# Two-block transformer kernel: first weights by k-slices behind the modulation rows, ring loads behind the last row, fourth recurrent gates one unit later

## The reference, cut to what matters

```python
c_act = jax.nn.silu(c)
mod = c_act @ mod_w[l] + mod_b[l]
sh1, sc1, g1, sh2, sc2, g2 = [m[:, None, :] for m in jnp.split(mod, 6, axis=-1)]
h = rms_norm(x, norm1_g[l]) * (1.0 + sc1) + sh1
proj = h @ w_in[l]
```

```python
xr = causal_depthwise_conv(xr, conv_w[l], conv_b[l])
r = jax.nn.sigmoid(block_diag_linear(x, w_a, b_a).astype(jnp.float32))
i = jax.nn.sigmoid(block_diag_linear(x, w_x, b_x).astype(jnp.float32))
log_a = -LRU_C * r * jax.nn.softplus(-lam.astype(jnp.float32))
a = jnp.exp(log_a)
u = jnp.sqrt(-jnp.expm1(2.0 * log_a)) * (i * xf)
```

## Time and profile before

| | |
|---|---|
| median of 3 runs | 3400.48 us (3400.35 to 3402.3) |
| profiled execution | 3401.0 us, of which the span of the profile 3399.3 us |
| TensorE (PE) busy | 3379.3 us, 99% |
| weight loads (PEld) | 2759.7 us, 81% |
| VectorE (DVE) | 1695.2 us, 50% |
| ScalarE (ACT) | 1316.7 us, 39% |
| GpSimd (POOL) | 1806.4 us, 53% |
| mean DMA rate | 100 GB/s; 391 to 426 GB/s from 4.5 to 36 us |

### The profile page before, as it was taken

How to read it: one execution, slowest core, us unless ns; L and a number is a source line. 1 busy time by engine, 2 the same in 40 slices (tenths; PEclk the granted TensorE clock), 3 DMA queues, 4 the chain that set the end, 5 groups by cost and what they waited for, 6 DMA issues and landing times.

```text
span 3399.3 us, 46823 instructions
## 1 busy us (share of the span) xinstructions
PE 3379.3 (99%) x15522; PEld 2759.7 (81%) x15522; DVE 1695.2 (50%) x2556; ACT 1316.7 (39%) x1820; POOL 1806.4 (53%) x2326
## 2 busy tenths in 40 slices
PE   9999999999999999999999999999999999999999
PEld 5888777888888887888888888888887888788887
DVE  8887775544553438614334434544368324243444
ACT  4365664222232226735633222322237545532222
POOL 6444435655555556553355555555556543465554
PEclk9999999999999999999999999999999999999999
DMA  5222552322222233231223223222223222223223
GB/s 218 88 68 69 174 168 99 110 95 99 93 99 94 97 99 106 93 99 63 69 94 106 97 94 99 93 99 96 95 93 118 93 74 69 81 93 99 99 93 111
DMA packets 93563, 339.59 MB, mean 100 GB/s; under 512 B 10497, under 2 KB 10881, under 8 KB 93314
## 3 DMA queue, kind: packets, MB, share of 16 engines
q1 hardware_dynamic: 86690, 313.16, 27.6%
q10 hardware_dynamic: 6752, 24.80, 2.4%
HBM read 331.62 MB, written 2.10 MB: 98 GB/s over the span
## 4 chain that ended last, share of the span: by engine, by line
PE 93%; DVE 3%; DVEq 1%; ACT 1%; DMA 1%; issue 1%; ACTq 0%; SPq 0%
PE ps L491 28%; PE ps L493 27%; PE ps L492 27%; PE ps L657 1%; PE ps L658 1%; PE ps L659 1%; PE ps L970 1%; PE ps L950 1%; PE ps L738 1%; DMA arena<-in_mod_w 1%; DVE arena L2112 1%; PE ps L961 1%; PE ps L598 0%; DVEq L2134 0%; DVE arena L2136 0%
## 5 line engine op out<-in xcount | busy, mean ns | idle before, releaser
L482 POOL TENSOR_TENSOR w_lo<-raw,w_hi 128x256 fp32r<-128x256 f32 x2268 | 1783.9, 818 | 1569.3 <-ACT w_hi L1057 1569.2
L1057 ACT ACTIVATE w_hi<-raw 128x1024 fp32r<-128x1024 f32 x569 | 599.2, 1056 | 1023.0 <-PE ps L493 1006.7
L491 PE MATMUL ps<-a_hi,w_lo 128*128 128x512 f32 x2216 | 875.0, 395 | 0.3 <-DVE a_lo L1773 0.3
L493 PE MATMUL ps<-a_hi,w_hi 128*128 128x512 f32 x2216 | 863.4, 390 | 0.0
L492 PE MATMUL ps<-a_lo,w_hi 128*128 128x512 f32 x2216 | 863.0, 389 | 0.0
L491 PE MATMUL ps<-b_hi,w_lo 128*128 128x512 f32 x2128 | 830.6, 390 | 4.2 <-DVE b_lo L1845 4.0
L492 PE MATMUL ps<-b_lo,w_hi 128*128 128x512 f32 x2128 | 829.1, 390 | 0.0
L493 PE MATMUL ps<-b_hi,w_hi 128*128 128x512 f32 x2128 | 829.0, 390 | 0.0
L491 PEld LDWEIGHTS ps<-a_hi,w_lo 128*128 128x128 f32 x2216 | 416.3, 188 | 98.2 <-issue 13.9
L493 PEld LDWEIGHTS ps<-a_hi,w_hi 128*128 128x128 f32 x2216 | 416.0, 188 | 88.3
L492 PEld LDWEIGHTS ps<-a_lo,w_hi 128*128 128x128 f32 x2216 | 416.5, 188 | 82.6 <-issue 0.5
(11 more groups left out here) (281 smaller groups left out, 2789.0 us busy)
## 6 DMA issues: line engine op xcount, KB each, us to landing
raw<-in_stream SPq DMA_DIRECT2D x570, 512.0 KB, 3.3
arena<-in_mod_w ACTq DMA_DIRECT2D x32, 512.0 KB, 4.0
arena<-in_mod_w SPq DMA_DIRECT2D x16, 512.0 KB, 11.5
arena<-arena ACTq DMA_DIRECT2D x16, 256.0 KB, 3.7
xres<-in_x_t SPq DMA_DIRECT2D x4, 512.0 KB, 5.0
xres<-in_x_t ACTq DMA_DIRECT2D x1, 2048.0 KB, 9.3
out_t<-xres SPq DMA_DIRECT2D x8, 256.0 KB, 2.0
arena<-in_first SPq DMA_DIRECT2D x3, 512.0 KB, 10.7
```

Source lines behind the costliest of these rows:

```text
L482: last = pool.tensor_tensor(w_lo[:, s, part], raw[:, s, part], w_hi[:, s, part].bitcast(F32), ALU.subtract)
L491: pe.matmul(out, lo, x_hi, start=start, stop=False)
L493: return pe.matmul(out, hi, x_hi, start=False, stop=stop)
L1057: act.activation(w_hi[:, slot, :], raw[:, slot, :], ACT.Copy).then_inc(hi_ready, 1)
```

## The change

Three things are changed.

The three first units are stored as eight slices, one for each k, each with the 128 columns of all three units (196,608 bytes). The load of slice k is issued behind the modulation loads 2k and 2k + 1, and TensorE waits for slice k in front of its matmuls for k. The three ring units 0 to 2 are all issued behind the last modulation load and the last slice. ScalarE's code is as it was.

`keep_columns` moves on VectorE from between the fourth and the fifth modulation load to behind the eight subtractions that make `a_lo`.

On TensorE, in each of the two layers, the fourth pair's `lru_gates(3)` moves from in front of the first output-gate tile to between the first and the second. ScalarE and VectorE keep their order.

```diff
-        first_w = area(ARENA - BRANCH, FIRST, D)
+        first_w = area(ARENA - BRANCH, KT, FIRST * P)
...
-        first_loaded, masks_ready, c_spread = sem("first_loaded"), sem("masks_ready"), sem("c_spread")
+        first_loaded = [sem(f"first_loaded{k}") for k in range(KT)]
+        masks_ready, c_spread = sem("masks_ready"), sem("c_spread")
...
             for n in range(MOD_FIRST):
                 load_mod(n)
-                if n == 3:
-                    for i in range(FIRST):
-                        sp.dma_start(first_w[:, i, :], first[i]).then_inc(first_loaded, 16)
-                if n == 13:
-                    load_raw(0)
-            load_raw(1)
-            load_raw(2)
+                if n % 2:
+                    sp.dma_start(first_w[:, n // 2, :], first[n // 2]).then_inc(first_loaded[n // 2], 16)
+            for s in range(RING):
+                load_raw(s)
...
-                pe.wait_ge(first_loaded, 16 * FIRST)
                 for k in range(KT):
+                    pe.wait_ge(first_loaded[k], 16)
                     pe.wait_ge(first_ready, k + 1)
-                    last = [pe.matmul(ps[:, bank, :], first_w[:, i, k * P:k * P + P], xres[:, k, :], start=k == 0, stop=k == KT - 1)
+                    last = [pe.matmul(ps[:, bank, :], first_w[:, k, i * P:i * P + P], xres[:, k, :], start=k == 0, stop=k == KT - 1)
...
                 units_of(bank_a)
+                project(bank_a())
                 lru_gates(3)
-                gates()
+                project(bank_a())
...
             for n in range(MOD_FIRST):
-                if n == 4:
-                    keep_columns()
...
                 low_part(a_lo[:, k, :], a_hi[:, k, :], xres[:, k, :]).then_inc(op_ready, 1)
+            keep_columns()
...
-        "first": np.ascontiguousarray(np.stack(early)),
+        "first": np.ascontiguousarray(np.stack(early).reshape(FIRST, P, KT, P).transpose(2, 1, 0, 3).reshape(KT, P, FIRST * P)),
```

## The result

The changed kernel takes **3408.5 us** (median of 20 executions, 3405.6 to 3410.2), the kernel before 3400.6 us (median of 20, 3400.1 to 3402.9). The ratio is 1.0021, 95% interval 1.0015 to 1.0027: 7.9 us or 0.23% slower. The forecast was 3405.2 us in a range of 3402.0 to 3409.5. The direction and the range hold; the size is 3.3 us short, and the result lies just beyond the bound of 0.2% under which the forecast counted it as the same. The profiled execution took 3408.8 us, its span 3407.0 us, 7.7 more than that of before.

A forecast was written before the change was run, and what follows sets the result against it. The prediction took TensorE, busy 99% of the span, as the bound. It summed 0.45 (start) + 0 (keep_columns) + 2.26 + 2.02 (gates, two layers) = +4.7 us, giving a median of 3405.2 us, range 3402.0 to 3409.5.

The forecast's parts named there:

- the bound of 0.2%: About 0.2% (6.8 us) is what measurement can tell from no change; a smaller difference counts as the same.
- ring unit 0 holds up k = 7: At the start, ScalarE rounds ring unit 0 before k = 7's scale; its landing at 36.1 makes the start +0.45 us.
- the 0.6 charged for the packets of 1536 B: In the DMA queue, eight slice loads cost 0.6 us beyond their bytes (0 to 1.3), moving ring unit 0 from 35.5 to 36.1.
- After that TensorE runs on: At the start, TensorE has no further wait after its last k, so the start ends at 38.27 in the kernel before.
- `keep_columns` costs nothing: On VectorE, the move delays the convolution chain 0.3 to 1.0 us, covered by slack: 0, bounds 0 to +0.5 us.
- the mechanism of the gates: In each layer, moved gates delay ScalarE's tanh, then its sigmoid, then TensorE's first query tile: +2.26 and +2.02 us.
- Bank wait: Before the first output-gate tile, TensorE waits 1.1 us for ScalarE's bank with a gelu tile, replacing the DMA wait.
- tanh's wait: On ScalarE, the fourth gates' tanh waits for the moved small matmuls and starts 2.34 us later in each layer.
- query tile's wait: Before the first query tile, TensorE waits 2.1 us for the bank that ScalarE's sigmoid of the output-gate tile frees.
- that rival: On ScalarE, the tanh's table load waits too: 1.28 us more in each layer, 3407.8 us; chance 0.07.
- the clock: Rival: TensorE's clock falls in new waits before query tiles and k = 7, 1.5 us each: 3406.7 to 3409.7; chance 0.22.
- a fall behind 3.2 us: In the earlier trace, TensorE waited 3.2 us before project_first and the clock was then 0.50; the new waits are shorter.

The follow-up runs named there:

- run 2: The changed kernel with lru_gates(3) and gates() back in their old place, so only the start is changed: 3401.0 us, ratio 1.0001.
- run 3: The changed kernel with two unused matmuls of ones filling TensorE's wait before the first query tile of each layer: 3406.2 us, ratio 1.0016.
- run 4: The changed kernel with ScalarE's sigmoid of the first output-gate tile and its tick put before the fourth gates' tanh: 3408.7 us, ratio 1.0023.
- run 8: The changed kernel's start, gates as before, with ScalarE rounding ring unit 0 only behind k = 7's shift: 3402.9 us, ratio 1.0005.
- run 9: The changed kernel's start, gates as before, with ring unit 0 loaded behind the fourteenth modulation load as in the kernel before: 3400.0 us, ratio 0.9998.
- run 1: The kernel before with only the fourth gates moved between the two output-gate tiles: 3407.8 us, ratio 1.0020.

## Why the prediction was right and where it fell short

**Right: ring unit 0 holds up k = 7.** Forecast at 36.1 with bounds from 35.5; ScalarE had it by 35.94. The Trainium skill (DMA: Bandwidth & Descriptors, Specifications) has 512 B as the size for line rate, which had given 35.5 here; in runs 2, 3 and 4, which have the same start, ScalarE had the unit at 35.60, 35.78 and 35.63. So the landing lies 0.1 to 0.4 us behind what bytes alone give, and the 0.6 charged for the packets of 1536 B was too much. (By its own rows, 6.6 less 6.2 is 0.4 and not 0.45 us, which makes the charge at most 0.9 instead of 1.3.) k = 7 came 0.2 us late, for 0.45 forecast.

**Missed: the start doesn't end at k = 7.** "After that TensorE runs on" was the failing step. The working followed ring unit 0 to ScalarE and stopped; the next in line, GpSimd, had 1.1 us of slack, was put back by 1.29, and took 1.0 longer for its four pieces. Runs 8 and 9 show it from both sides: k = 7 much earlier gives nothing, ring unit 0 earlier gives the start of before.

**Right: `keep_columns` costs nothing,** but not by the forecast's times. The subtractions took 7.03 us instead of 8.56 and ended at 42.3, not 44.0, and `keep_columns` took 2.2 us in its new place instead of 3.3. VectorE then waited 2.93 us for a gate that TensorE delivered later: the convolution chain started 0.97 later (48.30 for 47.33), as TensorE did. In run 9, where TensorE wasn't late, the move used up most of the slack: the chain ended at 152.10 for 151.61, 0.2 us ahead of `conv_mean`.

**Right: the mechanism of the gates.** Bank wait 1.12 (forecast 1.1), tanh's wait 2.54 (2.34), query tile's wait 1.90 (2.1), no table load in the way (it ran at 1398.13, ahead of the waiting tanh: that rival falls; in run 4 the load of the first sigmoid, which has two waits, did itself wait, 1.98 us, as the forecast's reading of the earlier trace rows has it). ScalarE caught up nowhere. The tile cost 5.66 us from its first matmul to the small ones, not 5.5, since the first matmul behind a wait holds the next up by 0.34 us instead of 0.23. With what follows, a layer came to 2.5 us for 2.26 and 2.02: 0.7 us too little together.

**Mis-sized: the clock.** The rival was named, with its place and its price (1.5 us; 1.6 measured), but given 0.22 and left out of the sum. Of the eight waits of 1.9 to 2.1 us in the profiles of the changed kernel and runs 1 to 4, five ended in half clock (in the layers two of two in the changed kernel and one of two each in runs 1 and 4; before k = 7 the one of run 2, and not the one of 2.06 us in run 3). The waits of 1.74 before k = 7 in the changed kernel and run 4 did not; the fill of run 3 took 2.3 us off the median. Of the 3.3 us that the forecast was short, 2.3 are the clock's and 0.7 the move's. The other 0.3 is less than medians can tell here; the start, which the profile shows at 0.98, came to 0.4 in the median of run 2, which is what had been forecast, though by another path. The argument that was wrong is the one that read the earlier trace rows, a fall behind 3.2 us, as a sign that 2.1 us would mostly pass. The range held because its upper end, 3409.5, did allow for two falls.

**Left open:** why the clock falls behind one wait of 1.9 us and not behind another of the same length. In run 1 the two layers do the same and differ in just this. The bank wait in front was 1.11 us in the layer that fell and 0.80 in the other, but the changed kernel's second layer fell behind one of 0.74.

## What to carry to other kernels

A step moved later on one engine must be followed through the engine that consumes it: here an in-order ScalarE held a finished tile behind a tanh that waited for the moved matmuls, and 1.8 us of waits for a DMA, which came back as waits for a bank, ended in 5 us of loss. Move it only as far as the consumer is busy with other work anyway (half a tile cost nothing, three quarters 0.7 us of waiting, though with ScalarE's first gelu moved forward too, a whole tile 2.5 us), and when a load is moved back in a queue, follow it through every engine that splits or copies it. Price each new wait of TensorE of some 2 us with the clock that it may lose as well.

## What was unexpected of the hardware

- The granted clock fell to 0.50 behind waits of only 1.9 to 2.1 us, in five of eight; a fall cost 1.5 to 1.6 us in the layers where it happened. Matmuls without use, 1.88 us of them in that gap, kept it at 1.00 in both layers. The Trainium skill (TensorE: Matmul & The Clock Gate, Part 1: The HAM clock gate) says that the clock is set by how busy TensorE has been; the filled run agrees, with 1.00 for 0.50 and 0.53 in the same stretches.
- GpSimd's subtraction of a 128 x 256 piece took 1.16 us in the changed kernel, four in a row beside VectorE's subtractions, which began at 35.29. In the kernel before, these began at 36.65: GpSimd's first two pieces (35.79 to 37.2) took 0.7 us each and the next two 1.17. The median of all its 2268 pieces is 0.74. The step in length falls where VectorE's subtractions begin; that they are the cause was not tried.
- An order that puts sigmoid in front of tanh cost one table load of 1.28 us more in each layer (run 4): 27 loads at the evacuations for 25 and 6 at the decay factors' exp for 4, with 2 fewer at the tanh.
- Eight loads of 197 KB in a queue of 512 KB loads cost the queue no more than their bytes, within 0.1 to 0.4 us (four profiles, 35.60 to 35.94 for 35.5).
